# Sample states of an mLSTM head read in column strips and updated in row strips of TensorE, four samples at a time

## The reference

```
p   = w_intra * einsum('bhtd,bhsd->bhts', q, k)
num = einsum('bhts,bhse->bhte', p, v) + w_state[..., None] * einsum('bhed,bhtd->bhte', C0, q)
den = jnp.sum(p, axis=-1) + w_state * jnp.einsum('bhd,bhtd->bht', n0, q)
h   = num / jnp.maximum(jnp.abs(den), jnp.exp(-m))[..., None]
C1  = w_last[..., None, None] * C0 + jnp.einsum('bhs,bhse,bhsd->bhed', ws, v, k)
n1  = w_last[..., None] * n0 + jnp.einsum('bhs,bhsd->bhd', ws, k)
```

## Time and profile before

| | |
|---|---|
| time, median of 3 runs | 1350.61 us (1348.88 to 1353.87) |
| the profiled execution's own time | 1349.3 us |
| its span | 1347.6 us |
| PE busy | 1303.0 us (97%), 8808 records |
| DVE busy | 748.4 us (56%) |
| ACT busy | 408.0 us (30%) |
| POOL busy | 60.4 us (4%) |
| mean granted clock of TensorE | 0.982 |

### The profile page before, as it was taken

One profiled execution on the slowest core, in us unless ns is written; L12 is line 12 of the kernel. 1 busy time (PEld: TensorE's weight loads), 2 busy tenths in 40 slices (PEclk: granted clock), 3 DMA queues, 4 the chain that ended last, 5 costly groups with the idle time before them and its releaser, 6 DMA issues.

```text
span 1347.6 us, 22251 instructions
## 1 busy us (share of the span) xinstructions
PE 1303.0 (97%) x8808; PEld 1279.7 (95%) x8808; DVE 748.4 (56%) x1304; ACT 408.0 (30%) x574; POOL 60.4 (4%) x56
## 2 busy tenths in 40 slices
PE   7999999999999999999999999699999999999996
PEld 7999999999999999899998999599999999999996
DVE  5633478778777878688655542663233324333333
ACT  5441233223223321221147234332123113213342
POOL 2000000000000000200000000480000000000000
PEclk9999999999999999999999999699999999999997
DMA  7152253243225322332322242022222222222211
GB/s 224 62 146 79 79 138 86 65 129 97 79 63 155 80 71 79 86 87 63 88 70 58 83 144 76 16 79 79 79 62 78 78 70 70 81 75 63 78 32 79
DMA packets 192158, 114.81 MB, mean 85 GB/s; under 512 B 13759, under 2 KB 189079, under 8 KB 192066
## 3 DMA queue, kind: packets, MB, share of 16 engines
q1 hardware_dynamic: 170882, 93.53, 24.7%
q10 hardware_dynamic: 21184, 20.02, 4.7%
HBM read 99.32 MB, written 14.21 MB: 84 GB/s over the span
## 4 chain that ended last, share of the span: by engine, by line
PE 92%; DVE 3%; ACT 3%; issue 1%; DMA 1%; SPq 0%; ACTq 0%; DVEq 0%; POOL 0%
PE out L351 78%; PE bank L1402 10%; PE bank L1397 4%; DMA WK<-in_x_prompt 1%; DVE WK L901 1%; DVE WK L904 1%; PE out L332 1%; ACT CV L532 1%; DVE XL L904 0%; ACT GH L532 0%; DVE WL L281 0%; ACT WK L532 0%; ACT WH L277 0%; ACT L532 0%; DVE CV L904 0%
## 5 line engine op out<-in xcount | busy, mean ns | idle before, releaser
L351 PE MATMUL out<-XH,WH 128*128 128x320 f32 (+1 forms) x1664 | 392.0, 317 | 12.7 <-DVE XL L904 8.9
L351 PE MATMUL out<-XH,WL 128*128 128x320 f32 (+1 forms) x1664 | 388.2, 315 | 0.0
L351 PE MATMUL out<-XL,WH 128*128 128x320 f32 (+1 forms) x1664 | 387.3, 314 | 0.0
L351 PEld LDWEIGHTS out<-XH,WH 128*128 128x128 f32 x1664 | 281.7, 190 | 16.2 <-issue 11.5
L351 PEld LDWEIGHTS out<-XH,WL 128*128 128x128 f32 x1664 | 282.8, 190 | 2.0 <-issue 1.3
L351 PEld LDWEIGHTS out<-XL,WH 128*128 128x128 f32 x1664 | 283.2, 190 | 0.9
L281 DVE TENSOR_TENSOR WL<-ST,WH 128x1024 fp32r<-128x1024 f32 x153 | 191.9, 1254 | 110.7 <-ACT WH L277 100.2
L904 DVE SCALAR_TENSOR_TENSOR CV<-WK,cwu,CV 128x512 f32 (+1 forms) x480 | 227.2, 543 | 0.4
L277 ACT ACTIVATE WH<-ST 128x1024 fp32r<-128x1024 f32 x153 | 161.3, 1054 | 190.9 <-PE out L351 183.2
L351 PE MATMUL out<-GH,WH 128*128 128x320 f32 x768 | 176.0, 310 | 6.0 <-DVE WL L281 4.6
L351 PE MATMUL out<-GH,WL 128*128 128x320 f32 x768 | 175.0, 309 | 0.0
(11 more groups left out here) (152 smaller groups left out, 617.7 us busy)
## 6 DMA issues: line engine op xcount, KB each, us to landing
ST<-in_w_in SPq DMA_DIRECT2D x65, 512.0 KB, 4.2
ST<-in_w_ff SPq DMA_DIRECT2D x64, 512.0 KB, 4.1
WK<-in_state_mlstm_C ACTq DMA_DIRECT2D x32, 256.0 KB, 3.2
o_C_sample<-WK ACTq DMA_DIRECT2D x32, 256.0 KB, 2.2
WK<-in_x_prompt SPq DMA_DIRECT2D x8, 512.0 KB, 6.1
ST<-in_w_branch_m SPq DMA_DIRECT2D x8, 512.0 KB, 4.6
ST<-in_w_branch_c SPq DMA_DIRECT2D x8, 512.0 KB, 4.1
ST<-in_w_out SPq DMA_DIRECT2D x8, 512.0 KB, 4.2
```

Of the source, the lines that this page charges most:

```text
L351: last = pe.matmul(out[s][:, h, 0:H], w[:, s, kk, :], x[:, kk, h * H:(h + 1) * H], start=(m < 2), stop=(m >= len(ms) - 2))
```

## The change

The mLSTM work is laid out anew, with the same products of the prompt:

- A group is four samples (first the odd ones 1, 3, 5, 7, then the even ones, table `BATCH`). Their transposed states have four places `c0t[0..3]` with n0 as 257th column. The transposes (into B7) of the first group stand after tiles 3 to 6, those of the second in slots 7 to 10.
- State read (`read_states`): q is now the stationary operand (128 rows, 32 columns in the first group, 16 in the second), the state with its 257 columns the moving one. The four samples' outputs are the four 32-partition strips of B4. 8 matmuls per group. For the odd samples q stands in a zeroed tile `qzo`.
- Update (D): the stationary operand is the 32 rows of `vwd` that hold one pair of samples (masked by parity), the moving one the same 32 rows of `ktok`. Four samples go to the four banks B4 to B7. 8 matmuls per group; DVE then makes the four additions.
- The prompt's normaliser is the 257th column of U (banks B6, B7) and not two matmuls of its own. The samples' numerator is summed by one matmul and the second group's reads in B4, and DVE adds the first group's result (`hti`).
- There are 13 slots. Each chunk's work stands in one slot (S of the next chunk, NUM, U). Stores and loads of sample states are issued four at a time. Row tables of the gates lie elsewhere, and the first head loads its states earlier.

```diff
-S_SLOT = {0: 0, 2: 1, 4: 2, 6: 3, 8: 4, 10: 5}
-NUM_SLOT = {1: 0, 3: 1, 5: 2, 7: 3, 9: 4, 13: 5}
-UPD_SLOT = {0: 0, 2: 1, 4: 2, 6: 3, 8: 4, 10: 5, 11: 6, 12: 7}
-TR_SLOT = {0: 0, 1: 1, 2: 2, 3: 3, 5: 4, 6: 5, 8: 6, 10: 7}
-INT_SLOT = {1: 0, 2: 1, 3: 2, 4: 3, 6: 4, 7: 5, 9: 6, 11: 7}
-NSLOT = 14
+NSLOT = 13
+S_SLOT = {0: 0, 2: 1, 3: 2, 4: 3, 5: 4, 6: 5}
+NUM_SLOT = {2: 0, 3: 1, 4: 2, 5: 3, 6: 4}
+D_SLOT = {1: 0, 11: 1}
+TR_SLOT = {7: 4, 8: 5, 9: 6, 10: 7}
+TR_TILE = {3: 0, 4: 1, 5: 2, 6: 3}
+N_SLOT, LAST_SLOT = 7, 12
+STORE_SLOT, LOAD_SLOT = 3, 5
+BATCH = [2 * g + 1 for g in range(C0RING)] + [2 * g for g in range(C0RING)]
...
-CONV_SLOT = {s: 2 if s % 2 else 3 for s in range(NSLOT) if 0 < s < 12}
+CONV_SLOT = {0: 3, 2: 3, 3: 3, 4: 2, 5: 3, 6: 2, 7: 3, 8: 3, 9: 3, 10: 2}
...
+            def c0t_copy(i, b):
...
+                copy(to[:, :, 0:DH], B7[:, :].rearrange("p (j e) -> p j e", j=2), "c0t_ready")
...
+                copy(to[:, :, DH:DH + 1], n0.rearrange("p j o b -> p (j o b)"), "c0t_ready")
...
+            def update_samples(i, g):
+
+                dve.wait_ge(sem("t_d"), 2 * i + g + 1)
+                for x in range(C0RING):
+                    b = BATCH[g * C0RING + x]
+                    dve.wait_ge(sem(f"c0_in{x}"), 16 * (2 * i + g + 1))
+                    stt(c0[:, x, :, :], c0[:, x, :, :], colH[:, 23 + b:24 + b],
+                        BK[x].rearrange("p (j e) -> p j e", j=2), ALU.mult, ALU.add).then_inc(sem("c1"), 1)
...
+            def read_states(i, g, start):
+
+                pe.wait_ge(sem("c0t_ready"), 2 * NB * i + 2 * C0RING * (g + 1))
+                for j in range(2):
+                    for x in range(C0RING):
+                        if g == 0:
+                            qs, L = qzo[:, j, 2 * LB * x:2 * LB * (x + 1)], 2 * LB
+                        else:
+                            qs, L = qw[:, j, NMETA + 2 * LB * x:NMETA + 2 * LB * x + LB], LB
+                        ins = mm(B4[2 * LB * x:2 * LB * x + L, 0:DH + 1], qs, c0t[x][:, j, :], start and j == 0, j == 1)
+                ins.then_inc(sem("t_num" if g else "t_int"), 1)
...
+                    elif c == 1:
+                        pe.wait_ge(sem("c1"), NB * i + C0RING)
...
+                    pe.wait_ge(sem("vws"), NPC * i + c + 1)
+                    for j in range(2):
+                        ins = mm(PB[1][:, j, 0:DH + 1], ktok[0:L, c, j * P:j * P + P], vws[0:L, :])
+                    ins.then_inc(sem("t_upd"), 1)
...
+                    for e in range(2):
+                        for x in range(C0RING):
+                            rows = slice(2 * LB * x, 2 * LB * (x + 1))
+                            ins = mm(BK[x][:, e * DH:(e + 1) * DH], vwd[rows, e * P:e * P + P], ktok[rows, SMP, :])
+                    ins.then_inc(sem("t_d"), 1)
+                if s == LAST_SLOT:
+                    pe.wait_ge(sem("c1"), NB * i + C0RING + 1)
+                    mm(B4[:, 0:DH + 1], pt[:, SMP % 2, :], vtok[:, SMP, :], True, False)
+                    read_states(i, 1, False)
```

More of the change, by code:

```diff
@@ L148, in build @@
     gcs = wk(off["vt"], KT * T2).rearrange("p (k t) -> p k t", k=KT)
-    assert off["c0t"] + KT * NB * PAD <= off["up"] and off["pt"] == off["hti"] + 256
+    assert off["c0t"] + KT * NB * PAD <= off["up"]
     z0 = off["so"] + 6 * D
@@ L695, in head @@
                 hi(n + 2)
-                if not first:
-                    states_in(i)
+                states_in(i)
                 evac(n + 1, two(k[:, 1, :]), scale=DH ** -0.5)
@@ L762, in head @@
                         evac(n + r, two(bcw), ACT.Sigmoid)
[L763 to L766, removed]
+                    if s == 0:
+                        act.wait_ge(sem("t_int"), i + 1)
+                        copy(hti, B4[:, 0:DH + 1], "hti")
+                    if s in NUM_SLOT:
+                        numer(i, NUM_SLOT[s])
+                    if s in TR_SLOT:
+                        c0t_copy(i, TR_SLOT[s])
+                    for g in range(C0RING):
+                        if s == STORE_SLOT:
+                            c1_store(i, g)
+                        if s == LOAD_SLOT:
+                            c0_load(i, C0RING + g)
+                    if s == N_SLOT + 1:
+                        act.wait_ge(sem("n1"), i + 1)
+                        act.dma_start(a["o_n_sample"][0, :, bass.ds(i, 1), :].rearrange("b o d -> b (o d)"), n0b[:, :]
+                                      ).then_inc(sem("n1_out"), 16)
+                for g in range(C0RING):
+                    c1_store(i, C0RING + g)
             def numer(i, c):
@@ L770, in numer @@
                 act.wait_ge(sem("t_num"), 6 * i + c + 1)
-                copy(num[0:L, c, :], B6[0:L, 0:257], "num")
+                copy(num[0:L, c, :], B4[0:L, 0:257], "num")
             head(0)
@@ L1114, in update, with weigh_v @@
[L1114 to L1124 removed]
+            def weigh_v(i, c):
+                wait(dve, "t_upd", NPC * i + c)
+                L = CHUNKS[c][1]
+                dve.tensor_scalar(vws[0:L, :], vtok[0:L, c, :], colH[0:L, 3 * c + 1:3 * c + 2], None,
+                                  ALU.mult).then_inc(sem("vws"), 1)
@@ L1609, in head @@
                         by_frame(vf, B6, 2)
+                    if r in TR_TILE:
+                        if r == 3:
+                            pe.wait_ge(sem("cache_sb"), KT)
+                            wait(pe, "u_sb", 3 * i)
+                        c0_by_key(i, TR_TILE[r])
                     if r == 7:
                         slot(i, 0)
-                slot(i, 13)
             head(0)
```

275 lines of the change are left out of this document (112 added, 163 removed).

## The result

The changed kernel takes 1298.07 us (median of 4 runs, 1297.37 to 1298.96), the kernel before 1350.44 us (4 runs, 1348.88 to 1353.87): ratio 0.9609, 95% interval 0.9589 to 0.9629. The span of the profiled execution went from 1347.6 to 1296.5 us, 51.1 less.

The account below looks back on a forecast made before the run. PE was taken to bound the kernel; per head 17.0 us removed and 8.5 + 0.8 + 0.6 = 9.9 added, 7.1 less, 28.4 over four heads, giving 1322 us. Own range 1316 to 1330, eight in ten 1308 to 1345.

Parts of the forecast that it names:

- What bounds the kernel: Whole kernel: PE, busy 97% of the span; work spared or given in the slots changes the time one for one.
- what is removed: Slots, per head: old state reads 7.1 us, U's one-column matmuls 2.2, D 6.9, slot 13's products 0.8; together 17.0.
- D: Old sample updates in the slots: removing 4 records at 0.217 us for each of eight samples saves 6.9 us per head.
- slot 13: Last slot work of a head: removing two identity products and two one-column ones saves 0.8 us per head.
- records start in program order: Read and update groups: only neighbouring strips' records overlap, 1.95 us per group of 8 matmuls; four groups 7.8 to 9.1, taken 8.5.
- an update group is held by its 16 weight loads: Updates, lower bound: 16 weight loads of 128 columns at 0.11 us take 1.8 us per group even with strips overlapping.
- rival 2: Read and update groups: all four strips at once, added 6.7 us, 10.3 less per head, 1309 us; chance 12%.
- the lower bound: Four groups per head with all four strips at once: 5.3 us, plus 0.8 us for changes of the array's shape.
- The Trainium skill's figure: Packed small matmuls: 3.07 times for four row strips; 13.9 us would become some 5.2 per head, another 13 us off.
- the wait in slot 2: Slot 2: PE's S waits for all four of DVE's additions; 0.45 us left plus 0.16 for pipe refill, 0.6 us per head.
- the shape's change: Read and update groups: changing the array's shape costs 0.1 us in and 0.1 out, four groups, 0.8 us per head.
- The range: Whole kernel's time: eight in ten between 1308 us, which holds rival 2, and 1345 us.

Follow-up runs that it names:

- The two parts put back: Changed kernel with, separately, the two one-column matmuls per chunk (1324.0 us) and the old state reads, 16 matmuls per group (1352.1 us), put back.
- the split wait: Changed kernel with slot 2 waiting for two of four additions ahead of the scores, all four only ahead of the prompt's update: 1296.3 us.

## Why the prediction was wrong

- **What bounds the kernel, what is removed:** right. The two parts put back cost 9.4 and 30 us where the terms said 8.8 and 28.4; the other two, D and slot 13, were not put back by themselves.
- **The step that failed:** "records start in program order; so only the second record of one strip and the first record of the next can be side by side", and with it the bound that "an update group is held by its 16 weight loads". Both were argued from one engine with one queue. In the runs each strip works off its own records, both passes and weight loads, whatever stands ahead for another strip: four starts near 0 apart, the sign that I had named for rival 2, and 4.3 us per head where 9.3 stood. That is 20 of the missing 23 us of span. Even the lower bound, 5.3 and 0.8, was too high by 1.8 us per head, all of it in the weight loads.
- **The Trainium skill's figure**, 3.07 times for four row strips ("TensorE: Matmul & The Clock Gate", Part 3), was much nearer; I gave it 12% since a matmul has two records here. The trace has 3.65 / 1.07 = 3.4 with the change of shape in it, and 3.45 / 0.87 = 4.0 without. The same page's rule that matmuls start in strict order of the program does not hold over strips here: 1.07 us issued in turns, 1.09 us strip by strip.
- **The sign of small terms:** the wait in slot 2 was 0.6 to 0.7 us (3.20 against 2.6 elsewhere, and against 2.50 once it was split) where 0.6 was forecast, the shape's change 0.2 per group. "TensorEngine Tiling (Array Packing)" of the Trainium skill says under PSUM Bottleneck that tiling does not speed up the emptying of PSUM. That wait bears it out, and the split wait shows that it was avoidable.
- **Not foreseen, in the change's favour:** PE's gap at two turns (2.7 us) and three clock dips, of which one came back elsewhere (2.6 us). Both were there to read: 62 instruction blocks on PE's queue in the page, some of them in every pass, for a body of 1,811 instructions, and 0.97 of clock in head 2's stretch against 1.00 in head 1's. I did not ask where the 1.5 us between these two stretches came from.
- **Not foreseen, against it:** DVE's longer gap, 0.8 us at two turns, 1.6 us.
- **The account:** 20 + 2.7 + 2.6 - 1.6, and 0.3 since head 0 waits less in slot 2, is 24 us; missing were 23 of span (51.1 against 28.4) and 24 of median. It closes within what a clock dip makes.
- **The range:** its lower end held rival 2, 1309, which had the same bound on weight loads in it. With the measured 4.3 and 0.6 the prediction's own sum gives 17.0 - 4.9 = 12.1 us less per head, 1302; the 4 us from there to 1298.1 are the terms not foreseen.

## What to carry to other kernels

Lay small matmuls to different strips whenever their operands allow it, and count the group as the work of its fullest strip plus 0.2 us; the order within it is free, fp32's two passes are no obstacle (all this for groups of 8 matmuls, as measured here). It can spare twice, since narrow matmuls one after the other were often followed here by stretches at half clock. Count the instructions of a loop body that PE turns in, and look at its instruction queue in one pass: none, or nine blocks and a gap of 1 to 5 us at each turn. Work moved from behind a turn to ahead of it has to be followed one wait further: here PE's wait only moved from one tile to the next.

## What the hardware showed that was not expected

- Sixteen fp32 records of 256 columns in one, two and four row strips: 3.65, 1.92 and 1.07 us. Column strips the same: +2.6 us per group when put into one.
- Starts did not follow the order of the program from one strip to another.
- A pure shift of PE's code by 80 instructions cost 11 us in a loop 900 us later. Bodies of 1,665, 1,705 and 1,767 instructions did not fetch, those of 1,747, 1,794, 1,811 and 1,863 did, with gaps of 0.9 to 4.9 us per turn; the 1,579 of the MLP's loop did or did not.
- DVE's gap at its turn is 2.8 and 3.8 us in the kernel before and about 5 us in most versions after. The extra time lies between the branch and the start of the fetch; its reason is still open.
